# A sparse-attention decoder layer: when the cached rows for compression are gathered, and where two low parts of weights are made

## The chip, the cores and the metric

The kernel runs on one core of a Trainium2 chip. The metric is the device time of one execution in microseconds (us). The profile names the engines PE (TensorE, matmuls), PEld (its weight loads), DVE (VectorE), ACT (ScalarE), POOL (GpSimd) and SP (SyncE). SP and POOL issue all the transfers; these run on 16 DMA engines that both share.

## The reference, cut to what matters

One layer of a hybrid decoder: a projection of 1024 prompt tokens and 8 x 4 sample tokens, three attention branches (compressed blocks, selected blocks, window), a short convolution, and an output projection. The change touches the compression and the output projection:

```
def compress(kv, pe, w1, w2):                      # kv: (b, l, heads, 64), blocks of 64 rows
    blocks = kv.reshape(b, l // BLK, BLK, g, d) + pe[None, None, :, None, :]
    flat = blocks.transpose(0, 1, 3, 2, 4).reshape(b, l // BLK, g, BLK * d)
    return jax.nn.silu(flat @ w1) @ w2             # w1: (4096, 128), w2: (128, 64)
...
    k_cmp, v_cmp = compress(full(past_kc, kc), ...), compress(full(past_vc, vc), ...)
...
    o = jnp.concatenate([o_attn * silu(z_a), y_conv * silu(z_c)], axis=-1) @ w_out
    x = x + gate[:, None, :] * o
```

`past_kc` and `past_vc` are pages of two caches, picked by a page table: 8 sequences of 2048 rows of 128 numbers each.

## The kernel before, in words

Five engines run programs of their own, joined by semaphores. Each engine, and each engine's list of transfers, goes in the order in which the program is written; nothing is reordered.

**Stages.** Conditioning and key/value projection; the large input projection in 24 blocks `n` (a fast matrix product: seven products `i` = 0 to 6 a block in all but the first three); compression (`turn`, `pair`); prompt attention (units `u`); sample attention in four pairs of sequences `pq` = 0 to 3; the output projection of nine tiles `tt`.

**Compression.** `c` = 0 is the keys, `c` = 1 the values. For each, the cached rows come as four quarters `q` into the buffers `xq[0]` to `xq[3]`; a quarter is two indirect transfers (`T` = 0, 1) of 128 rows of 8 KB, 2.1 MB together. `xq[0]` lies in the tile `near`, so the profile gives it that name. All of these buffers lie where operands of the input projection were, and `gather_quarter(0, 0)` waits for a product of the last block. PE's `turn(c, t)`, `t` = 0 to 63, transposes 16 turns out of each quarter (lines 1311 and 1312; every eighth pair of turns begins with the prompt's rows, `xp4`, lines 1308 and 1310). DVE and ACT copy what was turned into `xt` (lines 2347 and 1872), and `pair(c, m)`, `m` = 0 to 31, multiplies it with the weights `w1` (line 1318). `turn(0, 0)` waits for quarter 0 and for all of `xp4[0]` (`xp_ld[0]` at 192); `turn(0, 16)`, `turn(0, 32)` and `turn(0, 48)` wait for quarters 1, 2 and 3; the step `m` = 8 waits for the last three quarters of `w1[0]` (`xp_ld[2]`). The buffer `xt1`, first written at `m` = 4, lies over `qp`, so DVE and ACT wait there for all stores of queries (`q_st`).

**What SP issues around it.** The first quarter of `w1[0]`, `load_rows(0, r)` for `r` = 0 to 3 (the prompt's rows and the position table into `xp4[0]`, lines 723 and 725), three more quarters of `w1[0]` (line 718); then, behind waits for the last product, for `ych_st` and for `q_st`, the same for `c` = 1.

**What POOL issues around it.** In the last block: `gather_quarter(0, 0)` at `i` = 2, `store_za(23, 1)` at `i` = 5 (line 984), `store_q(23, 0)` at `i` = 6 (line 992, four transfers). After the block: `store_za(23, 0)`, `store_q(23, 1)`, a wait for product 6, `gather_quarter(0, 1)`; then ten waits, among them those for all stores; two stores out of `tailr` (lines 1046 and 1047); and the other quarters.

**The end of the sample attention.** PE: `turn_rows(2)`, `pair_values(2)` (line 1589, ends with `o5_mm` = 3), `turn_rows(3, range(3))`, `turn_o(2)` (line 1595, waits for `o5_cp`), `turn_rows(3, range(3, 6))`, `pair_values(3)`, then the output projection (line 1632), whose step `k` of tile 0 waits for `m_lo`, `wo_hi` and `wo_lo`. DVE runs the list at lines 2571 to 2594: `wo_low(j)` (line 2473) makes the low part `wol[j]` of a block of output weights from what ACT made at line 1950, `combine(pq)` (lines 2528 to 2535) joins the branches and releases `turn_o`, `gate_rows` and `last_row_copies` (line 2563) follow PE, and `mix_low(0)` (line 2570) makes the low part of tile 0 from what ACT made at line 1989. `early(2)` is `range(3, 5)`, so two `wo_low`.

Of the kernel before, what the change touches and what calls it, by code (L numbers as in the profile page):

```python
# [52 lines left out]
NBLK, NPLAIN, NSLOT = 24, 3, 5  # L53
# [12 lines left out]
def build(nc: "bass.Bass", x_prompt, x_sample, cache_k_cmp, cache_v_cmp, cache_k_slc, cache_v_slc, cache_k_win,  # L66
# [24 lines left out]
    def f32(ap):  # L91
        return ap.bitcast(F32)

    with ctx:
# [282 lines left out]
        def early(pq):  # L377

            return (range(0), range(0, 3), range(3, 5), range(5, 16))[pq]
# [136 lines left out]
        def plain(n):  # L516
            return n < NPLAIN

        def products(n):
            return 8 if plain(n) else 7  # L520

        def product(n, i):

            return 8 * min(n, NPLAIN) + 7 * max(0, n - NPLAIN) + i
# [88 lines left out]
        def act_at(n, name):  # L613
            return p2_act, place(ACT_EV, n, name)
# [4 lines left out]
        def made(n, i):  # L619
            return p2_mm, product(n, i) + 1  # L620
# [47 lines left out]
        def rows_of(tt):  # L668
            return P if tt < NTT - 1 else SAMP
# [244 lines left out]
        def _(po):  # L914
# [20 lines left out]
            def store_bias(q):  # L935

                rv = rows
                po.dma_start(rowd[:, 16 * q:16 * q + 16, :], bass.AP(rv.tensor, rv.offset, [list(rv.ap[0]), [0, 16], [1, XW]])).then_inc(row_st, 16)

            po.wait_ge(kv_ev, 2 * NTT)  # L940
            def store_rows(which):

                dst, col, t0 = ((p_kc, C_KC, 0), (p_vc, C_VC, 0), (p_ks, C_KS, 0), (p_vs, C_VS, 0), (p_kw, C_KW, 4), (p_vw, C_VW, 4))[which]
                src = kvc[:, :, col:col + DKV] if which < 2 else kvt[:, t0:8, col - KOFF:col - KOFF + DKV]
                po.dma_start(dst.rearrange("l b (t p) g d -> p (l b t) (g d)", p=P), src).then_inc(kc_st if which < 2 else out_st, 16)
                nout[0] += 0 if which < 2 else 16
# [17 lines left out]
            def gather_quarter(c, q):  # L964
                if c == 0 and q == 0:
                    po.wait_ge(*made(NBLK - 1, 1))
                cache = (cache_k_cmp, cache_v_cmp)[c]
                src = cache.rearrange("l n (e t) g d -> (l n e) (t g d)", e=8)
                for T in range(2):
                    po.indirect_dma_start(xq[q][:, T, :], None, src, bass.IndirectOffsetOnAxis(idxq[:, T, q:q + 1], 0)).then_inc(xq_ld[q], 16)  # L970
# [6 lines left out]
            def store_conv(n, half):  # L977

                po.wait_ge(*dve_at(n, f"h{half}"))
                po.dma_start(mixd[8 + n // 3, :, half, :], yy[:, half, :]).then_inc(ych_st, 16)  # L980

            def store_za(n, half):
                po.wait_ge(*act_at(n, f"za{half}"))
                po.dma_start(zad[n // 3, :, half, :], (er if half == 0 and not plain(n) else ca[half])[:, :]).then_inc(zab_st[half], 16)

            def store_q(n, half):
                j = n // 3
                po.wait_ge(*dve_at(n, f"l{half}"))
                for g in range(2):
                    own, head, cols = slice(64 * g, 64 * g + 64), 4 * (j // 2) + 2 * g + j % 2, slice(HT * half, HT * half + HT)  # L990
                    for a in range(2):
                        po.dma_start(f32(qst[head, 64 * a:64 * a + 64, cols]), f32(qp[own, 2 * half + a, 0:HT])).then_inc(q_st, 16)

            for n in range(NBLK):
                for i in range(products(n)):
                    if plain(n):
                        if n == 0 and i == 1:
                            po.wait_ge(ada_ev, 8)
                            po.dma_start(gbd, gate[:, :]).then_inc(g_st, 16)
                        if n == 2:  # L1000
                            if i == 0:
                                store_conv(1, 1)
                            if i == 1:
                                store_conv(1, 0)
                            if i == 5:
                                store_za(n, 1)
                            if i == 6:
                                store_q(n, 1)
                            if i == 7:
                                store_za(n, 0)  # L1010
                    else:
                        if n % 3 == 0 and i == 0 and n > NPLAIN:
                            store_za(n - 1, 0)
                        if n % 3 == 0 and i == 2:
                            store_q(n - 1, 0 if n == NPLAIN else 1)
                        if n % 3 == 1 and i == 6:
                            store_conv(n, 0)
                        if n % 3 == 2:
                            if i == 1:
                                store_conv(n - 1, 1)  # L1020
                            if i == 5:
                                store_za(n, 1)
                            if i == 6:
                                store_q(n, 0)
                    if i == 2 and 2 <= n < 6:
                        store_rows(n)
                    if n < 2 and i % 2:
                        po.wait_ge(*made(n, i - 1))
                        store_bias(4 * n + i // 2)
                    if n == NBLK - 1 and i == 2:  # L1030
                        gather_quarter(0, 0)
            store_za(NBLK - 1, 0)
            store_q(NBLK - 1, 1)
            po.wait_ge(*made(NBLK - 1, 6))
            gather_quarter(0, 1)
            po.wait_ge(w_lo, N_OPERANDS)
            po.wait_ge(out_st, nout[0])
            po.wait_ge(ych_st, 32 * 8)
# [9 lines left out]
            for c in range(2):  # L1048
                for q in range(4):
                    if 4 * c + q >= 4:  # L1050
                        po.wait_ge(x3_t, 16 * (4 * c + q - 3))
                    if 4 * c + q >= 2:
                        gather_quarter(c, q)
            for q in range(4):
                po.wait_ge(xq_ld[q], 2 * 32)
# [976 lines left out]
        def _(dve):  # L2032
# [300 lines left out]
            for c in range(2):  # L2333
                for m in range(32):
                    n = 32 * c + m
# [135 lines left out]
            def wo_low(j):  # L2471
                dve.wait_ge(wo_hi, j + 1)
                dve.tensor_tensor(wol[j][:, :], wor[j][:, :], f32(woh[j][:, :]), ALU.subtract).then_inc(wo_lo, 1)
# [52 lines left out]
            def combine(pq):  # L2526
                dve.wait_ge(e5, pq + 1)
                link(dve.reciprocal(i5[:, :], r5[:, pq % 2, :]))
                link(dve.tensor_tensor(i5[:, :], i5[:, :], gr[:, pq, 1:3], ALU.mult))
                dve.wait_ge(o5_mm, pq + 1)  # L2530
                link(dve.tensor_scalar(o5[:, :], PS[:, 5, P:2 * P], i5[:, 0:1], None, ALU.mult))
                link(dve.scalar_tensor_tensor(o5[:, :], PS[:, 5, 2 * P:3 * P], i5[:, 1:2], o5[:, :], ALU.mult, ALU.add))
                dve.scalar_tensor_tensor(o5[:, :], PS[:, 5, 3 * P:4 * P], gr[:, pq, 0:1], o5[:, :], ALU.mult, ALU.add).then_inc(o5_cp, 1)
                dve.wait_ge(o5_cp, pq + 1)
                dve.sem_inc(b5_rd, 1)
# [22 lines left out]
            def last_row_copies():  # L2558
                dve.wait_ge(o5_mm, 3)
                for q in (1, 3, 5):  # L2560
                    n = 58 + q
                    dve.wait_ge(t5, n + 1)
                    dve.tensor_copy(pt5[:, 4 * q - 4:4 * q, :], PS[:, group_bank[n], :].rearrange("p (a c) -> p a c", a=4)).then_inc(ev5d, 1)

            def mix_low(tt, halves=(0, 1)):
                n = rows_of(tt)
                for a in halves:
                    dve.wait_ge(m_hi, 2 * tt + a + 1)
                    ks = slice(8 * a, 8 * a + 8)
                    dve.tensor_tensor(ml[:, ks, 0:n], mr[:, ks, 0:n], f32(mh[:, ks, 0:n]), ALU.subtract).then_inc(m_lo, 1)  # L2570
# [4 lines left out]
            for pq in range(2):  # L2575
# [4 lines left out]
                for j in early(pq):  # L2580
                    wo_low(j)
                pair_rows(pq + 2)
            for j in early(2):
                wo_low(j)
            combine(2)
            gate_rows(2)
            last_row_copies()
            mix_low(0)
            for j in early(3):
                if j == 10:  # L2590
# [106 lines left out]
```

## Time and profile before

| what | value |
|---|---|
| median of 3 runs | 1491.7 us (1487.86 to 1492.43) |
| the profiled execution | 1485.97 us |
| its span | 1484.2 us |
| PE busy | 1421.5 us, 96% of the span |
| DVE busy | 960.4 us, 65% |
| share of the 16 DMA engines' span | q1 23.1%, q0 15.1% |

The span is that of one profiled execution, from its first to its last record; its own device time is 1.8 us longer. q1 carries what SP issues, q0 what POOL issues. Shares of busy time are means over all stages; what a wait costs is read in its own stage.

### The profile page before, as it was taken

What the parts mean: (1) busy time and instruction counts of PE and PEld (TensorE: products, weight loads), DVE (VectorE), ACT (ScalarE), POOL (GpSimd) and SP (SyncE); (2) the same over time, 40 slices, a digit from 0 to 9 for tenths busy, and PEclk for the clock granted to TensorE, in tenths of its full rate; (3) what the DMA queues carried; (4) which work ended last, traced back from release to release, by engine and by line L of the source; (5) the groups of instructions that cost most, each with busy time, mean ns of one, the idle gap of its engine ahead of it and who ended that gap; (6) DMA issues with size and microseconds to landing.
All of it is one profiled execution on the core that took longest, in us unless ns stands there. A gap on an engine that the chain in (4) does not pass through costs nothing.

```text
span 1484.2 us, 27910 instructions
## 1 busy us (share of the span) xinstructions
PE 1421.5 (96%) x10526; PEld 1226.2 (83%) x10526; DVE 960.4 (65%) x2309; ACT 705.1 (48%) x1546; POOL 236.9 (16%) x447
## 2 busy tenths in 40 slices
PE   5999999999999999989989989989989999899998
PEld 1889999999999999977777777777777766688886
DVE  2646878878788787767676576576676563743226
ACT  2433233232322333266677777777777755621111
POOL 1101120110100101131021242232231141000000
PEclk9999999999999999999999999999999999999999
DMA  9335733332333423597221221221121049963321
GB/s 347 111 111 106 119 115 87 93 109 46 105 82 90 116 48 97 142 349 232 60 87 35 71 74 42 57 66 44 38 58 30 22 164 317 279 181 99 88 86 36
DMA packets 169862, 164.76 MB, mean 111 GB/s; under 512 B 53757, under 2 KB 150269, under 8 KB 164353
## 3 DMA queue, kind: packets, MB, share of 16 engines
q1 hardware_dynamic: 153904, 94.11, 23.1%
q0 software_dynamic: 15824, 68.87, 15.1%
q8 instruction: 84, 1.38, 0.4%
q14 instruction: 50, 0.40, 0.1%
HBM read 131.27 MB, written 35.83 MB: 113 GB/s over the span
## 4 chain that ended last, share of the span: by engine, by line
PE 88%; DVE 4%; DMA 3%; ACT 2%; issue 2%; SPq 1%; POOL 0%; DVEq 0%; ACTq 0%
PE PS L1266 33%; PE PS L1632 12%; PE PS L1438 8%; PE PS L1403 7%; PE PS L1382 5%; PE PS L1318 4%; PE PS L1383 4%; PE PS L1223 2%; PE PS L1224 2%; PE PS L1225 2%; DMA kwb<-in_cache_k_win 1%; DMA adaw<-in_ada_w 1%; PE PS L1485 1%; PE PS L1547 1%; PE PS L1414 1%
## 5 line engine op out<-in xcount | busy, mean ns | idle before, releaser
L1266 PEld LDWEIGHTS PS<-bo,wsl 128*128 128x128 f32 x4104 | 499.4, 188 | 0.4 <-issue 0.4
L1266 PE MATMUL PS<-bo,wsl 128*128 128x264 f32 x4104 | 499.6, 284 | 0.0
L1893 ACT ACTIVATE pr<-PS,nm 128x640 f32<-128x640 f32 (+7 forms) x256 | 181.3, 709 | 44.8 <-DVE nm L2395 42.2
L1728 ACT ACTIVATE wsl<-wsum 128x512 fp32r<-128x512 f32 x105 | 65.6, 631 | 237.8 <-DVE wsum L2118 237.8
L1916 ACT ACTIVATE ptt<-PS 128x512 f32<-128x512 f32 x264 | 149.8, 601 | 39.6 <-PE PS L1403 39.4
L1403 PE MATMUL PS<-ident,pr 128*128 128x128 f32 x1056 | 146.6, 273 | 0.3 <-ACT ptt L1916 0.3
L1438 PE MATMUL PS<-ptt,kvt 128*64 128x256 f32 x1056 | 136.2, 389 | 0.0
L1403 PEld LDWEIGHTS PS<-ident,pr 128*128 128x128 f32 x1056 | 122.1, 141 | 9.2 <-issue 0.6
L1438 PEld LDWEIGHTS PS<-ptt,kvt 128*64 128x64 f32 x1056 | 66.8, 136 | 41.1 <-issue 16.4
L2395 DVE CUSTOM_DVE_ANT_0 PS<-PS,near,nm 128x256 f32<-128x256 f32 x192 | 94.7, 493 | 6.8
L2394 DVE TENSOR_REDUCE nm<-PS 128x1 f32<-128x128 f32 (+5 forms) x128 | 70.5, 551 | 38.8 <-PE PS L1383 38.2
L2124 DVE TENSOR_TENSOR wsl<-wsum,wsl 128x512 fp32r<-128x512 f32 x105 | 70.9, 692 | 29.7 <-ACT wsl L1728 29.5
L1382 PE MATMUL PS<-ksh,qb 128*128 128x384 f32 (+3 forms) x192 | 75.9, 397 | 11.8 <-ACT pr L1893 10.5
L1632 PE MATMUL PS<-woh,mh 128*128 128x512 f32 x256 | 79.4, 391 | 0.0
L1632 PE MATMUL PS<-wol,mh 128*128 128x512 f32 x256 | 79.0, 390 | 0.0
L1632 PE MATMUL PS<-woh,ml 128*128 128x512 f32 x256 | 78.9, 389 | 0.0
L2570 DVE TENSOR_TENSOR ml<-mr,mh 128x1024 fp32r<-128x1024 f32 x16 | 19.6, 1226 | 90.7 <-ACT mh L1989 90.6
L1382 PE MATMUL PS<-kwh,qb 128*128 128x384 f32 (+3 forms) x192 | 70.8, 370 | 6.9 <-ACT pr L1893 6.9
L1318 PE MATMUL PS<-xt,w 128*128 128x273 f32 x256 | 72.1, 404 | 4.9 <-DVE xt L2347 2.6
L2118 DVE TENSOR_TENSOR wsum<-wr 128x512 f32<-128x512 f32 x105 | 68.5, 685 | 1.2 <-DMA wr<-in_w_in 1.2
L2347 DVE COPY xt<-PS 64x256 f32<-64x256 f32 x128 | 54.0, 422 | 23.3 <-PE PS L1312 19.5
L1989 ACT ACTIVATE mh<-mr 128x1024 fp32r<-128x1024 f32 x16 | 17.0, 1061 | 100.7 <-PE PS L1632 100.0
(358 smaller groups left out, 2422.0 us busy)
## 6 DMA issues: line engine op xcount, KB each, us to landing
wr<-in_w_in SPq DMA_DIRECT2D x32, 512.0 KB, 5.6
adaw<-in_ada_w SPq DMA_DIRECT2D x8, 1024.0 KB, 9.4
wr<-in_w_in SPq DMA_DIRECT2D x32, 256.0 KB, 4.5
q_stacked<-qp POOLq DMA_DIRECT2D x64, 128.0 KB
qb<-q_stacked SPq DMA_DIRECT2D x32, 256.0 KB, 3.0
mr<-mixed SPq DMA_DIRECT2D x16, 512.0 KB, 3.8
mixed<-yy POOLq DMA_DIRECT2D x16, 264.0 KB
xb<-in_x_prompt POOLq DMA_DIRECT2D x8, 512.0 KB, 4.5
```

The lines of the kernel that those rows point to most:

```text
L1266: ins = pe.matmul(PS[:, 2 * q + c, 0:H // 2], w[:, x, kk, :], b[:, y, kk, c * H // 2:(c + 1) * H // 2], start=(first and kk == 0 and x == ...
L1318: ins = pe.matmul(PS[:, 4 + g, 0:CB], w1[c][:, m, :], xt[m // 4 % 2][:, m % 4, g, :], start=(m == 0), stop=(m == 31))
L1382: pe.matmul(PS[:, b0 + c, x:x + m], q, kh[:, g, a:a + m], start=True, stop=False)
L1403: ins = pe.transpose(PS[:, turn_bank(c), h * P:(h + 1) * P], pr[w % 3][:, h, t * P:(t + 1) * P], ident[:, :])
L1438: ins = pe.matmul(PS[64 * g:64 * g + 64, 6, a:a + 2 * P], v, pt[tc % NPT5][:, 2 * g:2 * g + 2, :].rearrange("p j c -> p (j c)"), start=(t ...
L1632: ins = pe.matmul(PS[0:n, b0 + c, :], a[:, k, 0:n], b[k][:, 512 * c:512 * c + 512], start=(k == 0 and a is mh and b is woh), stop=(k == 15 ...
L1893: act.activation(pr[r][:, h, 0:k], score_cols(b0, w), ACT.Exp, scale=-1.0, bias=nm[:, r, h:h + 1], accum_out=rsum[:, r, h:h + 1]).then_inc ...
L1916: act.activation(pt[tc % NPT5][:, :, :], PS[:, turn_bank(c), :].rearrange("p (h c) -> p h c", h=4), ACT.Copy).then_inc(pt_act, 1)
L2118: dve.tensor_tensor(wsum[(sums_to(m) - 1) % 2][:, :, :], raw(*a), raw(*b), op).then_inc(w_sum, 1)
L2124: dve.tensor_tensor(wsl[m % NSLOT][:, 1, :, :], source(m), f32(wsl[m % NSLOT][:, 0, :, :]), ALU.subtract).then_inc(w_lo, 1)
L2394: link(dve.tensor_reduce(low, cols[:, 0:far], AX.X, ALU.min))
L2395: dve.tensor_tensor_reduce(cols[:, far:k], cols[:, far:k], near[:, head_of(u, h), 2 * P - (k - far):2 * P], 1.0, low if far else 3.0e38, A ...
```

## The change

Two things are moved; no work is added or left out.

- POOL: `gather_quarter(0, 1)` goes from behind the last product to the place `i` = 5 of the last block, behind a wait for product 4 alone; quarters 2 and 3 of the keys go from behind the stores' waits and the two `tailr` stores to the place where quarter 1 was. The values' quarters stay where they are.
- DVE: the two `wo_low` of `early(2)` go from in front of `combine(2)` to behind `last_row_copies()`, in front of `mix_low(0)`.

```
@@ -1029,10 +1029,14 @@
                     if n == NBLK - 1 and i == 2:
                         gather_quarter(0, 0)
+                    if n == NBLK - 1 and i == 5:
+                        po.wait_ge(*made(n, 4))
+                        gather_quarter(0, 1)
             store_za(NBLK - 1, 0)
             store_q(NBLK - 1, 1)
             po.wait_ge(*made(NBLK - 1, 6))
-            gather_quarter(0, 1)
+            gather_quarter(0, 2)
+            gather_quarter(0, 3)
             po.wait_ge(w_lo, N_OPERANDS)
             po.wait_ge(out_st, nout[0])
@@ -1049,7 +1053,7 @@
                 for q in range(4):
                     if 4 * c + q >= 4:
                         po.wait_ge(x3_t, 16 * (4 * c + q - 3))
-                    if 4 * c + q >= 2:
+                    if c:
                         gather_quarter(c, q)
@@ -2580,11 +2584,11 @@
                 pair_rows(pq + 2)
-            for j in early(2):
-                wo_low(j)
             combine(2)
             gate_rows(2)
             last_row_copies()
+            for j in early(2):
+                wo_low(j)
             mix_low(0)
```

## Rows read from the trace of the kernel before

**Rows 1.** The page: PE busy, and the chain by engine.

```profile
PE 1421.5 (96%) x10526; PEld 1226.2 (83%) x10526; DVE 960.4 (65%) x2309; ACT 705.1 (48%) x1546; POOL 236.9 (16%) x447
...
PE 88%; DVE 4%; DMA 3%; ACT 2%; issue 2%; SPq 1%; POOL 0%; DVEq 0%; ACTq 0%
```

**Rows 2.** Waits of PE, whole span: us in total, times, longest.

```profile
PE PS L1595 <- DVEq L2535: 2.0, 1, 2.0
...
PE PS L1308 <- DMA xp<-in_cmp_pe_k: 1.3, 1, 1.3
```

**Rows 3.** Timeline of POOL, 608 to 645: start, us, what, [idle before].

```profile
615.80 1.04 POOL L970 DMA_INDIRECT near<-in_cache_k_cmp,idxq  x1 [0.35 <-issue]
617.14 1.41 POOL L970 DMA_INDIRECT near<-in_cache_k_cmp,idxq  x1 [0.30 <-issue]
622.18 0.59 POOL L984 DMA_DIRECT2D z_attn_silu<-ca  x1 [3.63 <-ACT ca L1739]
625.84 2.14 POOL L992 DMA_DIRECT2D q_stacked<-qp  x4 [3.06 <-DVE qp L2196]
...
633.53 1.01 POOL L970 DMA_INDIRECT xq<-in_cache_k_cmp,idxq  x1 [0.30 <-issue]
...
639.24 0.57 POOL L1046 DMA_DIRECT2D out_p_cv<-tailr  x1 [3.41 <-DMA q_stacked<-qp]
```

**Rows 4.** DMA queues, 622 to 626: packets, MB, share of 16 engines.

```profile
q0 software_dynamic: 123, 1.00, 83.5%
q1 hardware_dynamic: 356, 0.23, 22.1%
```

**Rows 5.** DMA queues, 626 to 632.

```profile
q1 hardware_dynamic: 1504, 0.88, 82.5%
q0 software_dynamic: 153, 0.47, 29.6%
```

**Rows 6.** DMA queues, 638 to 642.

```profile
q0 software_dynamic: 216, 1.64, 99.2%
q1 hardware_dynamic: 117, 0.05, 4.8%
```

**Rows 7.** The chain, 600 to 765: start, us, what.

```profile
625.23 6.59 DMA xp<-in_cmp_pe_k
```

**Rows 8.** Timeline of PE, DVE and ACT, 624 to 650.

```profile
631.96 0.30 PE L1308 MATMUL PS<-ident,xp 128*128 128x128 f32 x1 [1.33 <-DMA xp<-in_cmp_pe_k]
...
634.23 2.16 PE L1318 MATMUL PS<-xt,w 128*128 128x273 f32 x4 [0.98 <-ACT xt L1872]
...
640.52 0.46 DVE L2345 COPY xt<-PS 64x68 f32<-64x68 f32 x2 [0.61 <-PE PS L1312]
...
645.03 1.09 PE L1318 MATMUL PS<-xt,w 128*128 128x273 f32 x4
...
646.69 0.86 DVE L2347 COPY xt<-PS 64x256 f32<-64x256 f32 x2 [2.18 <-PE PS L1312]
...
647.65 0.70 PE L1318 MATMUL PS<-xt,w 128*128 128x273 f32 x2 [0.83 <-DVE xt L2347]
```

**Rows 9.** Busy time by stretch: PE, PEld, DVE, ACT, POOL, PEclk, DMA share, GB/s.

```profile
634.00:638.00 4.00, 3.77 (x14) 3.18 (x15) 1.04 (x3) 0.94 (x4) 1.53 (x2) 0.57 1.10 370
...
1286.00:1290.00 4.00, 4.00 (x36) 3.34 (x36) 2.18 (x3) 2.67 (x4) 0.00 (x0) 0.57 1.13 348
```

**Rows 10.** Timeline of PE, 1262 to 1310.

```profile
1273.85 1.15 PE L1485 MATMUL PS<-ident,s 128*128 128x128 f32 x8 [0.19 <-ACT pt L1945]
...
1280.08 0.38 PE L1589 MATMUL PS<-vcs,pt 32*64 32x128 f32 x4
...
1283.82 0.30 PE L1595 MATMUL PS<-ident,o 128*128 128x128 f32 x1 [2.04 <-DVEq L2535]
...
1285.72 1.71 PE L1485 MATMUL PS<-ident,s 128*128 128x128 f32 x8 [1.16 <-DVE pt L2563]
...
1293.78 0.74 PE L1632 MATMUL PS<-woh,mh 128*128 128x512 f32 x2
```

**Rows 11.** Timeline of DVE, 1262 to 1310.

```profile
1279.82 2.36 DVE L2473 TENSOR_TENSOR wol<-wor,woh 128x1024 fp32r<-128x1024 f32 x2 [3.87 <-ACT woh L1950]
...
1282.49 0.35 DVE L2531 TENSOR_SCALAR o<-PS,i 128x128 f32<-128x128 f32 x1
...
1287.47 0.69 DVE L2563 COPY pt<-PS 128x512 f32<-128x512 f32 x1 [1.21 <-PE PS L1485]
1288.31 1.23 DVE L2570 TENSOR_TENSOR ml<-mr,mh 128x1024 fp32r<-128x1024 f32 x1
```

**Rows 12.** Timeline of ACT, 1262 to 1310.

```profile
1287.22 1.06 ACT L1989 ACTIVATE mh<-mr 128x1024 fp32r<-128x1024 f32 x1
```

**Rows 13.** Line 783 (last loads of window values, issued 1259.8 and 1260.1).

```profile
DMA to landing us min/median/max: 22.3/22.9/23.4
```

**Rows 14.** DMA queues, 632 to 638.

```profile
q1 hardware_dynamic: 2099, 1.06, 58.8%
q0 software_dynamic: 415, 1.20, 50.9%
```

More of the change, by code:

```diff
@@ L1031, in _ @@
                         gather_quarter(0, 0)
+                    if n == NBLK - 1 and i == 5:
+                        po.wait_ge(*made(n, 4))
+                        gather_quarter(0, 1)
             store_za(NBLK - 1, 0)
@@ L1034, in _ @@
             po.wait_ge(*made(NBLK - 1, 6))
-            gather_quarter(0, 1)
+            gather_quarter(0, 2)
+            gather_quarter(0, 3)
             po.wait_ge(w_lo, N_OPERANDS)
@@ L1051, in _ @@
                         po.wait_ge(x3_t, 16 * (4 * c + q - 3))
-                    if 4 * c + q >= 2:
+                    if c:
                         gather_quarter(c, q)
@@ L2582, in _ @@
                 pair_rows(pq + 2)
-            for j in early(2):
-                wo_low(j)
             combine(2)
@@ L2587, in _ @@
             last_row_copies()
+            for j in early(2):
+                wo_low(j)
             mix_low(0)
```

## The prediction

> **What bounds the kernel now.** The page comes first: PE is busy for 1421.5 of 1484.2 us and the chain lies on PE for 88% [rows 1]. PE's work isn't changed, so only its idle time and its clock can move: 62.7 us of idle time over the whole span, of which a change of order can reach a few. The waits of PE come second [rows 2]: they show which part of the change stands beside a wait. One wait, 2.0 us on DVE's line 2535, is the release of `turn_o(2)`, in front of which the two `wo_low` stand. No wait of PE names a quarter of the cached rows; the only wait on a transfer at the start of the compression is 1.3 us for `xp4`, which the diff doesn't touch. The third view, the timelines and the DMA queues around both places, gives the prices.
>
> **Part one, the quarters.** POOL's time first. Product 4 of the last block ends about when DVE starts on it, and POOL's `store_za(23, 1)` is issued until 622.77; then POOL is idle for 3.06 us until `store_q(23, 0)` [rows 3]. Two indirect transfers take 1.04 to 1.41 us each with 0.3 us ahead of them, so 2.7 to 3.4 us: quarter 1 fits in that hole, at a cost of 0 to 0.4 us to the stores behind it. Quarters 2 and 3 take four times 1.3 us from 633.5, until 638.8; POOL reached the first `tailr` store at 639.24, after waiting 3.41 us for the query stores [rows 3], so that issue is hidden too. What is now behind them in POOL's list, the `tailr` stores, is waited for by nothing until the end of the compression.
>
> What quarter 1 gains: `turn(0, 16)` follows `pair(0, 6)`. In the trace `pair(0, 7)` starts 2.62 us after it (645.03, 647.65), where 1.36 us is the pitch of the steps that wait for nothing (1.09 us of matmuls and two turns), and DVE stood idle for 2.18 us on PE's transposes [rows 8]. Something held PE for about 1.3 us where it comes to quarter 1, issued at 633.5 to 635.8 and so in flight for some ten us. I take it that this is the arrival of quarter 1, and that it goes: -1.3 us. The bound is 0, since the view names DVE and not the transfer. Quarters 2 and 3 gain nothing: PE shows no such hole at `turn(0, 32)` or `turn(0, 48)`.
>
> What quarter 1 costs. It puts 2.1 MB on q0 from 623 to 626, while the transfers of `xp4[0]`, with which PE starts, are on q1. The last of these is issued at 625.23 and takes 6.59 us [rows 7]; PE starts at 631.96 after its 1.33 us [rows 8], so any delay is PE's in full. The queues share the engines: while quarter 0 (8 KB rows) was on q0, q0 had 83.5% and q1 22.1%; once it was over, q1 had 82.5% [rows 4, 5]; and with quarter 1 alone q0 moved 1.64 MB in 4 us [rows 6]. So 2.1 MB take 5.1 us of all engines; while they run q1 keeps 22%, and the last of `xp4` comes 5.1 x 0.78 = 4.0 us later. Bounds: 0, if q1's packets hold their pace beside quarter 1, and 6.2 us, if q0 runs at the 1.00 MB in 4 us of [rows 4] (8.4 us for 2.1 MB, in which q1 does 1.9 of the 5.8 x 0.825 = 4.8 us of work that it has left at 626, and 3.6 us more for the rest, which makes 638.0). I take +4.0.
>
> The Trainium skill, "DMA: Bandwidth & Descriptors", section "Queues, rings and completion order", says that each DMA engine takes turns between the queues at packet granularity. By that rule, too, a queue of large rows holds up one of small rows, and it speaks against moving 2.1 MB in front of `xp4`; it gives no other sum.
>
> The clock: from 634 to 638 it stood at a mean of 0.57, 1.2 in place of 2.4 GHz for most of it, after the wait at line 1308 [rows 8, 9]; 4 us at 0.57 lose 1.7 us. If PE starts 4 us later, a stretch of the same length at the same place falls into waiting, and gives 1.7 us back; if it is longer or starts later, nothing. I take -0.8, with bounds of -1.7 and +1.7.
>
> Further waits that may come late. `q_st`: its stores are behind 2.1 MB more on q0; they were done before 639.24, DVE asks at 640.52, which moves to 644.5 [rows 3, 8]. So +0, up to +2 if they are later by over 5 us. `w1[0]`, q1: asked for at `m` = 8, near 649, without a wait. It now has quarter 1 in front of it and 4.2 MB of quarters 2 and 3 right behind the stores; beside such rows q1 had 4.8% [rows 6]. I take +0.5, bounds 0 and +3.
>
> Sum of part one: -1.3 + 4.0 - 0.8 + 0.5 = +2.4 us.
>
> **Part two, the low parts.** DVE was ready at 1275.95, waited 3.87 us for ACT's `woh`, and ran the two `wo_low` for 2.36 us; `combine(2)` read its first accumulator at 1282.49, and PE, idle for 2.04 us, went on at 1283.82 [rows 10, 11]. Without them `combine(2)` waits for `pair_values(2)` alone, which ends at 1280.46. From the first read to PE's start are 1.33 us, so PE starts at 1280.5 + 1.33 = 1281.85 and gains 1.95 us. The next wait, 1.16 us on the copies of `last_row_copies`, moves along as it is. Behind this, the clock: 0.57 from 1286 to 1290, after six us in which PE waited twice; eight transposes took 1.71 us where they took 1.15 before [rows 9, 10]. That cost 1.7 us. With one of the two waits gone I take it that it doesn't fall: -1.5 (bounds -1.7 and 0). The two `wo_low` now stand in front of `mix_low(0)`. DVE's last copy ended at 1288.16 and ends near 1285.6; two `wo_low` of 1.22 us end near 1288.1, and `mix_low(0)` can't start before ACT is done with `mh` at 1288.28, begun at 1287.22 [rows 11, 12]. So they are hidden, `m_lo` comes at 1289.6, and PE is there at 1293.78 - 3.45 = 1290.3. Without that cover they'd cost up to 2.4 us. `pair_values(3)` now starts near 1284.9, and the last values land at 1260.1 + 23.4 = 1283.5 [rows 13]: not late. Sum of part two: -3.4 us, between -1.9 and -3.7.
>
> **Sum.** +2.4 - 3.4 = -1.0 us on the profiled execution, 1485.97 to 1485.0 us. That execution is 5.7 us under the median of 1491.7 and 1.9 us under the lowest of the runs shown, so I take the difference over to the median: 1490.7 us.
>
> **The rivals.**
> - No measurable change (forecast): the parts cancel within 4.5 us. Within 0.3%, 4.5 us, is what a measurement of this kernel can't tell from none; the runs shown differ by that much.
> - Crowded out, slower: the place is `turn(0, 0)`. Quarter 1 holds `xp4` for the full 6.2 us, the same queue holds `w1[0]` for 3 us more at `m` = 8, the clock gives nothing, and part two gives 1.9: 6.2 + 3 - 1.3 - 1.9 = +6.0, 1497.7 us. For it: q1's 4.8% [rows 6]. Against: PE came to `m` = 8 without a wait. It decides once part one costs over 7.9 us, or over 6.4 with part two at its least.
> - Faster: `xp4` isn't held (cost 0), the hole at quarter 1 and both low stretches of the clock go: -1.3 - 1.7 - 3.5 = -6.5, 1485.2 us. For it: between 632 and 638, with stores and the first of quarter 1 on q0, both queues ran side by side at 58.8% and 50.9% [rows 14]. Against: [rows 4], where the large rows were alone on q0.
> - The change does nothing: both moves are hidden, since PE waits for no quarter by name and `combine(2)` waits for another thing. 1491.7 us, inside the forecast. Against: the 2.04 us [rows 2, 10].
>
> **How the numbers follow.** Forecast and the last rival together 0.62, crowded out 0.15, faster 0.23. The likeliest case's own range is 1487 to 1495. The range reaches to both outer cases: 1485.5 to 1497 leaves out the tails beyond them, and the scatter of the runs. Chances: faster by over 0.3% 0.22, within 0.63, slower 0.15.
>
> **What the profile would show.** `xq` for keys issued near 623, right behind line 984, and four more from 633.5; PE's wait at line 1308 grown from 1.3 to about 5 us, its first turn near 636; `pair(0, 7)` 1.4 us after `pair(0, 6)`; no wait of PE on line 2535, `turn_o(2)` right behind the transposes; no fall of the clock before the output projection, and DVE's `mix_low(0)` starting where it did relative to `mh`. Wrong it would be if line 1308 waits no longer than before (then faster), or if PE waits at `m` = 8 for `w1` or at line 1632 for `mix_low`.

## The result, and the profile after

The changed kernel takes 1493.44 us (median of 20 runs, 1489.7 to 1497.86) where the kernel before takes 1490.22 us (20 runs beside it, 1483.9 to 1493.15): ratio 1.003, 95% interval 1.002 to 1.0041, so 4.5 us slower (3.0 to 6.1). It stands at the edge of what was called no change, on the side that was given 0.15. The profiled execution took 1493.26 us, with a span of 1491.5 us. It is 7.3 us over the profiled execution of the kernel before, more than the 4.5 us of the runs, since that one was 4.3 us under its own median.

The waits of PE over the whole span of the changed kernel (us in total, times, longest), beside [rows 2]:

```profile
PE PS L1312 <- DMA xp<-in_cmp_pe_k: 7.1, 1, 7.1
...
PE PS L1489 <- DMA kb<-in_cache_k_slc,idxs: 2.1, 1, 2.1
...
PE PS L1315 <- DMA w<-in_cmp_w_k: 1.7, 1, 1.7
```

The wait on `combine(2)` is gone (the lines have moved by 4). The wait for `xp4` (line 1308 before, 1312 now) went from 1.3 to 7.1 us, and there is a new one for `w1` at `m` = 8.

The timeline of POOL, beside [rows 3]:

```profile
622.70 0.59 POOL L984 DMA_DIRECT2D z_attn_silu<-ca  x1 [3.66 <-ACT ca L1743]
623.59 0.97 POOL L970 DMA_INDIRECT xq<-in_cache_k_cmp,idxq  x1 [0.30 <-issue]
624.86 0.95 POOL L970 DMA_INDIRECT xq<-in_cache_k_cmp,idxq  x1 [0.30 <-issue]
626.36 2.19 POOL L992 DMA_DIRECT2D q_stacked<-qp  x4 [0.55 <-DVE qp L2200]
...
642.01 0.57 POOL L1050 DMA_DIRECT2D out_p_cv<-tailr  x1 [3.21 <-DMA q_stacked<-qp]
```

Quarter 1 is issued ten us earlier, and the stores behind it are issued on time: POOL still waits 0.55 us for DVE in front of them. Issuing costs nothing. The last store of queries was through at 642.0 in place of 639.2, and only POOL waited for it, no longer than before.

The timeline of PE, beside [rows 8] (the first turn, pairs 0, 3, 6 and 7, and the step `m` = 8):

```profile
638.21 0.45 PE L1312 MATMUL PS<-ident,xp 128*128 128x128 f32 x1 [7.07 <-DMA xp<-in_cmp_pe_k]
...
641.14 2.16 PE L1322 MATMUL PS<-xt,w 128*128 128x273 f32 x4 [0.56 <-ACT xt L1876]
...
648.34 1.09 PE L1322 MATMUL PS<-xt,w 128*128 128x273 f32 x4
...
652.72 1.09 PE L1322 MATMUL PS<-xt,w 128*128 128x273 f32 x4
...
654.30 1.09 PE L1322 MATMUL PS<-xt,w 128*128 128x273 f32 x4
657.04 0.33 PE L1315 MATMUL PS<-ident,xq 128*128 128x128 f32 x1 [1.65 <-DMA w<-in_cmp_w_k]
```

Busy time by stretch of the changed kernel (columns as in [rows 9]):

```profile
632.00:636.00 4.00, 0.00 (x0) 0.00 (x0) 0.47 (x1) 0.00 (x0) 3.39 (x6) 0.55 1.02 333
636.00:640.00 4.00, 1.79 (x9) 1.82 (x10) 0.85 (x3) 0.22 (x2) 2.20 (x3) 0.50 1.06 399
640.00:644.00 4.00, 3.44 (x12) 2.48 (x11) 1.29 (x4) 1.73 (x5) 1.12 (x2) 0.50 1.03 416
644.00:650.00 6.00, 5.95 (x32) 4.94 (x30) 3.30 (x9) 3.40 (x10) 0.00 (x0) 0.83 1.04 416
```

The clock fell while PE stood idle, as before, but it stayed at 1.2 GHz until about 646, eight us into the work. And the DMA queues (packets, MB, share of 16 engines), 628 to 636, while PE stands idle for `xp4`, then 632 to 638, 638 to 642 and 642 to 648:

```profile
q0 software_dynamic: 355, 2.35, 89.8%
q1 hardware_dynamic: 381, 0.24, 13.2%
...
q0 software_dynamic: 407, 1.91, 88.7%
q1 hardware_dynamic: 409, 0.22, 13.9%
...
q0 software_dynamic: 340, 1.47, 90.6%
q1 hardware_dynamic: 339, 0.17, 14.7%
...
q0 software_dynamic: 320, 2.33, 93.9%
q1 hardware_dynamic: 317, 0.16, 9.4%
```

The first column is what the prediction didn't look at: both queues have work, and each moves as many packets as the other, or nearly. q0's are mostly 8 KB rows (6.6 and 7.3 KB in the mean from 628 to 636 and from 642 to 648; 4.3 KB from 638 to 642, with stores among them), q1's 0.5 to 0.6 KB, so by bytes q0 gets about nine tenths.

The loss in this pair of traces can be laid out along PE's time. The tails come 0.51 us later in this trace (629.60 and 630.11), which is not the change's; against that offset:

| mark | later by, us | what was added |
|---|---|---|
| first turn | 5.74 | the wait for `xp4` |
| pair 3 | 7.19 | 1.45, the low clock |
| pair 7 | 6.14 | -1.05, the hole at quarter 1 closed |
| first pair behind the wait for `w1` | 7.49 | 1.35 |
| first scores of the prompt attention | 7.46 | 0 |
| output projection | 6.83 | -0.6, the low parts less other waits |

### The profile page after: what moved, and what is told of

Read it like the earlier page. It is cut to its first block, busy times and chain, and to the rows that moved or that the text cites. A ratio compares the mean times of both kernels' runs of the same rounds, so it can differ in the third digit from the quotient of the medians.

```text
span 1491.5 us, 27910 instructions
## 1 busy us (share of the span) xinstructions
PE 1423.5 (95%) x10526; PEld 1229.4 (82%) x10526; DVE 960.6 (64%) x2309; ACT 704.5 (47%) x1546; POOL 235.9 (16%) x447
## 4 chain that ended last, share of the span: by engine, by line
PE 86%; DMA 4%; DVE 4%; ACT 2%; issue 2%; SPq 1%; POOL 0%; DVEq 0%; ACTq 0%
PE PS L1270 33%; PE PS L1636 12%; PE PS L1442 8%; PE PS L1407 7%; PE PS L1386 5%; PE PS L1387 3%; PE PS L1322 3%; PE PS L1227 2%; PE PS L1228 2%; PE PS L1229 2%; DMA w<-in_cmp_w_k 2%; DMA kb<-in_cache_k_slc,idxs 1%; PE PS L1489 1%; DMA adaw<-in_ada_w 1%; PE PS L1593 1%
## 5 line engine op out<-in xcount | busy, mean ns | idle before, releaser
L1387 PE MATMUL PS<-ksl,qb 128*128 128x384 f32 (+3 forms) x192 | 64.1, 343 | 0.0
```

The costliest lines, as they stand in the source:

```text
L1387: ins = pe.matmul(PS[:, b0 + c, x:x + m], q, kl[:, g, a:a + m], start=False, stop=True)
```

## The experiments

Times are ratios to the kernel before, run beside on the same chip, with 95% intervals. 0.1% is 1.5 us.

**The quarters alone.** The changed kernel with the two `wo_low` back in front of `combine(2)`:

```
-            combine(2)
-            gate_rows(2)
-            last_row_copies()
             for j in early(2):
                 wo_low(j)
+            combine(2)
+            gate_rows(2)
+            last_row_copies()
```

> The quarters' part alone; the low parts stay in front of combine(2). Theory A (quarter 1 crowds out xp4): PE's first turn waits about 7 us for xp4, then about 1.7 us for w1 at m = 8, and half of the clock's low stretch falls on work: +7 to +8 us in the trace between the last product and the end of the compression, and +5 to +8 us in the time. Theory B (the loss seen came from elsewhere, such as the wait of 2.1 us for a key gather in the sample attention, and the quarters cost little): 0 to +3 us.

Measured: 1.0057 (1.0037 to 1.0078), so 8.5 us slower (5.5 to 11.6); waits of 6.5 us for `xp4` and 2.0 us for `w1`; the first scores 7.0 us later against the tails. Theory A, and B is out: this trace has no wait for a key gather in the sample attention at all.

**The low parts alone.** The kernel before with the second half of the diff:

> The low parts' part alone. Both theories: no wait of PE on combine(2) (2.0 us before) and PE at the output projection about 2 us earlier from turn_o(1) on; 3.4 us if the clock doesn't fall behind it. In the time -1.5 to -4 us. A rival, that the two wo_low now delay mix_low(0): 0 us, with a wait of PE at line 1632.

Measured: 0.9963 (0.9951 to 0.9976), so 5.5 us faster (3.6 to 7.3). PE's wait on `combine(2)` is gone; none on `mix_low` came. The gain is more than the 1.5 to 4 us expected. Within their intervals the two parts add up: +8.5 - 5.5 = +3.0, where both together gave +4.5 (3.0 to 6.1).

**Quarter 1 alone, and quarters 2 and 3 alone.** In the first, only this is added to the kernel before, with `gather_quarter(0, 1)` taken from its old place; in the second, quarter 1 stays and the other two follow it at once (and go from their old place):

```
# e3
+                    if n == NBLK - 1 and i == 5:
+                        po.wait_ge(*made(n, 4))
+                        gather_quarter(0, 1)
# e4
             po.wait_ge(*made(NBLK - 1, 6))
             gather_quarter(0, 1)
+            gather_quarter(0, 2)
+            gather_quarter(0, 3)
```

> Only quarter 1 is issued early; quarters 2 and 3 stay behind the waits for the stores. Theory A: the whole wait at line 1308 is here (6.5 to 7.5 us), the wait for w1 at m = 8 may be gone; +5 to +7 us in the time. Theory C (it is all 6.3 MB together that hold up q1): the wait at line 1308 is under 4 us and the time +1 to +3 us.

> Quarter 1 stays behind the last product, quarters 2 and 3 are issued right behind it, in front of the waits for the stores. Theory A: the wait at line 1308 is 1.3 us as before, since nothing is added to q0 before 633; w1 comes later and PE may wait for it at m = 8, 0 to 3 us: 0 to +3 us in the time. Theory C: +3 to +6 us.

Measured: quarter 1 alone 1.0029 (1.0016 to 1.0042), so 4.3 us slower (2.4 to 6.3), somewhat less than was expected, with 6.1 us of wait for `xp4` and none for `w1`; quarters 2 and 3 alone 1.0005 (0.9988 to 1.0022), 0.7 us of wait for `xp4`. The wait for `xp4` is quarter 1's. The two don't add up to the quarters' 8.5 us; but the intervals are wide enough to hold the 3.4 us left over. Part of it is the wait for `w1` of 1.7 to 2.0 us, which is in both traces with all three quarters moved and in neither of these. The second trace names a wait at quarter 1, which the trace of the kernel before did not (waits of PE, 610 to 760):

```profile
PE PS L1310 <- DMA xq<-in_cache_k_cmp,idxq: 1.2, 1, 1.2
PE PS L1310 <- DMA xp<-in_cmp_pe_k: 0.7, 1, 0.7
```

**Half of quarter 1.** Only the first of its two transfers is early, the second at the old place:

```
-            def gather_quarter(c, q):
+            def gather_quarter(c, q, halves=(0, 1)):
...
+                        gather_quarter(0, 1, (0,))
...
             po.wait_ge(*made(NBLK - 1, 6))
-            gather_quarter(0, 1)
+            gather_quarter(0, 1, (1,))
```

> The dose: only the first of quarter 1's two transfers (1.05 MB) is early, the second stands where quarter 1 was, and quarters 2 and 3 as before. Theory A by bytes: PE's wait at line 1308 lies half way between 1.3 and 6.3 us, 3 to 5 us. A theory in which any large row on q0 starves q1 until the stores are through gives 6 us as with the whole quarter; one of a threshold gives 1.3.

Measured, one run of 1493.28 us: a wait of 4.1 us. With 1.3 us for nothing early, 4.1 for 1.05 MB and 6.1 for 2.1 MB, the wait grows with the bytes in front.

**The rows first.** In the changed kernel, and in the kernel with the low parts alone, the rows of `xp4` go in front of the first quarter of `w1[0]`:

```
-            load_w1(0, 0, wr_ld)
             sp.wait_ge(kc_st, 32)
             for r in range(4):
                 load_rows(0, r)
+            load_w1(0, 0, wr_ld)
```

> The changed kernel, with load_rows(0, r) issued in front of the first quarter of w1[0]. Theory A (quarter 1's 2.1 MB hold up whatever of q1 is still due): the wait only moves, from xp4 (7.1 us) to w1 at the first pair; pair 0 starts 0 to 2 us earlier than in the changed kernel and the time is 0 to -2 us against it, so +2 to +5 us against before. Theory D (xp4 is slow for its own small rows and its order behind w1): xp4's wait falls under 3 us, nothing takes its place, and the time is no more than +1 us against before.

> The low parts' part with the quarters as before, and load_rows(0, r) in front of the first quarter of w1[0]. Nothing of quarter 1 is on q0 here before 633. Theory D: the 1.3 us of wait at line 1308 go, so -1 to -1.5 us against e2_lowparts. Theory A: w1's first quarter becomes the one that comes last, 0 to +1 us against e2_lowparts. Either way between -4 and -7 us against before.

Measured in the changed kernel: 1.0085 (1.0057 to 1.0113), worse than either theory had it. Waits of PE, 610 to 765:

```profile
PE PS L1315 <- DMA w<-in_cmp_w_k: 11.5, 1, 11.5
PE PS L1312 <- DMA xp<-in_cmp_pe_k: 3.6, 1, 3.6
```

`xp4` came earlier by 3.5 us. But `w1`'s first 512 KB, which were in before PE asked for them in the changed kernel, were now in only at 648.7, and pair 0 began at 649.59. What of q1 is left when quarter 1 begins goes one packet for each of q0's, until q0 runs out of 8 KB rows; there are 1024 packets of 512 bytes in a quarter of `w1` and 256 rows in a quarter of the cache. With the low parts alone the same order of loads did nothing: 0.9969 (0.9948 to 0.999), pair 0 at 632.85, no wait for `xp4` or `w1`, and a wait of 2.0 us for quarter 1 in their place.

**PE kept busy.** To take the clock away from the wait:

```
             tails()
+            for k in range(56):
+                pe.transpose(PS[:, 5, 0:P], ident[:, :], ident[:, :])
             turn(0, 0)
```

> The changed kernel with 56 transposes of the identity (about 6 us of PE) between tails and turn(0, 0), into a bank that pair 0 overwrites: it separates the wait from the clock. The transfers are the same, so the first turn starts within 0.5 us of where it does in the changed kernel. If the clock is a price of its own, the first four steps run at the full clock, pair 7 comes 3 to 4 us earlier, and the time is -2 to -4 us against the changed kernel unless w1 at m = 8 then takes it back as a longer wait (1.7 us now, 4 to 5 us then), in which case the time is the same.

Measured: 1.0049 (1.0026 to 1.0073), so nothing won. The clock held at 1.00 until pair 6, which came at 647.79 in place of 652.72. But (timelines of POOL and PE):

```profile
648.61 1.00 POOL L970 DMA_INDIRECT near<-in_cache_v_cmp,idxq  x1 [6.45 <-PE PS L1316]
...
663.98 0.48 PE L1315 MATMUL PS<-ident,xq 128*128 128x128 f32 x1 [13.52 <-DMA w<-in_cmp_w_k]
```

PE was through quarter 0 earlier, POOL gathered the values' first quarter at 648.61 in place of 653.53, and this closed the gap in q0 in which `w1` had landed. In the wait of 13.5 us the clock fell after all, from 654 to 667, the last 3.5 us of it on work. So this run doesn't take the clock's price out of the time; it moves it to the next wait. **The same with that gather held back:**

```
+                    if 4 * c + q == 4:
+                        po.wait_ge(xp_ld[2], 48)
                     if c:
                         gather_quarter(c, q)
```

> The kernel of e7 (changed kernel, PE kept busy), with the values' quarter 0 issued only once w1[0] has landed whole. Theory E (while 8 KB rows are on q0 the engines take one packet of each queue in turn, so 512-byte packets of w1 get through only one for each 8 KB row; in e7 the values' quarter, issued at 648.6, closes the hole in q0 in which w1 would have landed): PE's wait at m = 8 falls from 13.5 us to 5 to 8 us, w1 lands near 657, and the time is 5 to 7 us under e7. Theory F (w1 is late for its own sake, by the rate of 512-byte packets): the wait stays over 11 us.

Measured: 1.0022 (1.0000 to 1.0043), and a wait of 7.4 us in place of 13.5, as theory E has it; theory F is out. The time is 4.0 us under that with PE kept busy alone, where 5 to 7 were expected, and the two intervals overlap, so the times by themselves don't show the gain. The queues from 648 to 654 in this kernel:

```profile
q1 hardware_dynamic: 2132, 1.11, 76.6%
q0 software_dynamic: 155, 0.68, 28.0%
```

With few rows on q0, q1 moves 2132 packets in six us, where it moved 310 from 642 to 648.

**The opposite of the change.** With the low parts, quarter 1 held until `w1[0]` is in:

```
             po.wait_ge(*made(NBLK - 1, 6))
+            po.wait_ge(xp_ld[2], 48)
             gather_quarter(0, 1)
```

> The low parts' part, and the opposite of the change to the quarters: quarter 1 is issued only once w1[0] has landed whole. Theory E: without 8 KB rows on q0, w1 is through near 638 to 640 in place of 646 to 647; quarter 1 takes 5 to 6 us and lands near 645 to 646, where PE asks for it, so the hole of 1.3 us there is gone or is now a wait of 0 to 2 us for quarter 1; quarters 2 and 3 are still in time. 0 to -2 us against the low parts alone. Theory F: w1 is as late as before, quarter 1 comes after 651 and PE waits for it over 4 us: +4 us or more.

Measured: 1.0000 (0.9985 to 1.0015), a miss: 3.3 to 5.5 us above the two measurements of the low parts alone. `w1` was in at 640.2, but that was hardly a gain: in the kernel before, q1 moved only 16 packets from 640 to 642 beside 116 of q0, so it had little left by then, and the expectation's 646 to 647 was wrong. And PE then waited:

```profile
PE PS L1309 <- DMA xq<-in_cache_k_cmp,idxq: 6.4, 1, 6.4
```

Quarter 1, issued from 640.23, took eleven us to land and not five to six. The `tailr` stores and the other quarters were issued right behind it; that they are the reason was not tested. Both ends are bad; the place where the kernel before has this gather lies between them.

**PE kept busy for 1.3 us, and the low parts again.** The same loop with 12 in place of 56 on the kernel with the low parts, and that kernel once more:

> The low parts' part with 12 transposes of the identity (1.3 us) in the wait at line 1308. If the clock's fall at the start of the compression is a price of its own: it comes later or not at all, and 1 to 3 us against the low parts alone. Theory E's objection: PE then comes sooner to m = 8 and waits for w1, so nothing is gained (0 to +1 us).

> The kernel of e2 again, to set e10 and e11 beside it on the same chip: 0.9963 of before again within 0.0015, PE's wait on combine(2) absent.

Measured: 0.9965 (0.9947 to 0.9982) and 0.9978 (0.9952 to 1.0003): no difference. With the short loop PE waited 2.9 us for quarter 1. The low parts alone remain the best version, at 0.9963 and 0.9978, though the second interval just reaches the kernel before. Their second trace is the one in which nothing else happened near the end of the sample attention, so the prediction's second part can be read from it (timeline of PE):

```profile
1281.16 0.30 PE L1595 MATMUL PS<-ident,o 128*128 128x128 f32 x1
...
1289.55 0.73 PE L1632 MATMUL PS<-woh,mh 128*128 128x512 f32 x2
```

## Why the prediction was wrong, step by step

**POOL's issue, right.** Quarter 1 fitted in the hole, quarters 2 and 3 too; `q_st` wasn't waited for late.

**The hole at quarter 1, right in size, not in what it was due to.** Taken at -1.3 us, measured -1.05. Waits of 1.2 to 2.9 us for `xq` in four experiments with quarter 1 at its old place show that PE can come there too early. But in the first trace of the low parts, with quarter 1 at its old place too, PE came to pair 6 at 646.28 in place of 645.03, and pair 7 followed 1.58 us later, without a hole and as in the changed kernel (timeline of PE, pairs 6 and 7):

```profile
646.28 1.09 PE L1318 MATMUL PS<-xt,w 128*128 128x273 f32 x4
...
647.86 1.09 PE L1318 MATMUL PS<-xt,w 128*128 128x273 f32 x4
```

A PE that comes a little over one us later has no hole, moved or not. The prediction itself made PE 4 us late at `xp4`, and that alone would have closed the hole: the -1.3 belongs in the sum, but as part of the delay and not as a gain of the early issue. That the hole in the trace of the kernel before was quarter 1's arrival is likely, not shown.

**The wait for `xp4`, mis-sized: the first of the two terms that failed.** Taken at +4.0 with bounds of 0 and 6.2, measured at +5.7. The step was "2.1 MB take 5.1 us of all engines; while they run q1 keeps 22%". Both halves were too kind. q0 moved 2.35 MB in the eight us from 628 to 636, nearer the rate of [rows 4] than that of [rows 6], and q1 had 13.2% of the engines meanwhile. The 22% was read in [rows 4], where q0 moved 123 packets and q1 356: by these counts it was no stretch of two full queues. In one, q1 has as many packets as q0, and 9 to 15% in the stretches shown above. The kernel before shows this too: in the second half of [rows 4] itself, 624 to 626, and later, from 654 to 660 and from 660 to 666.

```profile
q0 software_dynamic: 70, 0.57, 88.5%
q1 hardware_dynamic: 82, 0.06, 11.4%
...
q0 software_dynamic: 251, 1.82, 92.6%
q1 hardware_dynamic: 251, 0.13, 9.8%
...
q0 software_dynamic: 324, 2.37, 96.7%
q1 hardware_dynamic: 324, 0.07, 5.9%
```

**The clock, wrong in sign: the second, and by size the larger miss.** Taken at -0.8, measured +1.45, so 2.25 us off where `xp4` was 1.7. The step was "a stretch of the same length at the same place falls into waiting". A longer wait didn't swallow the low stretch, it made it longer: 634 to 638 before, 632 to 646 now. The experiments agree: the stretch at 1.2 GHz behind the wait for `xp4` was absent after waits of 0.7 and 0.9 us, nought to 7 us long after 1.3 to 1.5, 7 us after 4.1 and 10 to 14 us after 6.1 to 7.1; with PE kept busy in place of the wait it was absent there. What its removal would be worth in the time was not measured, as the run with PE kept busy only came sooner to `w1` and lost the clock there.

**`w1` at `m` = 8, too small.** Taken at +0.5, measured +1.35, within its bounds. All of part one is then +7.5 in place of +2.4. That is the rival "crowded out", by its own mechanism, with less of a wait for `w1` than it had and a price of the clock that it left out; it had 0.15 and 1497.7 us. I gave each term its middle, although the clock hangs on the wait for `xp4`, and that wait and the one for `w1` on the same shares of the same queues, so that they move together.

**The low parts, right.** Taken at -3.4. From `turn_o(1)` to the output projection PE gained 3.54 us in the trace of the low parts' second run (-0.69 to -4.23 against before), of it 1.97 at `combine(2)`, and the clock didn't fall; the times gave -5.5 and -3.3 us. From `turn_o(2)` to the output projection PE took 8.4 us in all nine traces with the part, at the full clock, and 9.9 to 11.5 in the five without it, where the clock fell behind the wait. `mix_low` hid the two `wo_low`. In the changed kernel's own trace the gain from `turn_o(1)` on was 1.69 us: a wait of 2.1 us for a key gather stood in front, with a low stretch of the clock behind. Such a wait, 0.7 to 3.4 us, is in eight of the fourteen traces and absent from the others, with and without either part; what decides it was not found.

**The sum.** -1.0 us was forecast and +4.5 measured; the traces give +7.5 for the quarters and -1.7 to -3.5 for the low parts. 1493.44 us lies in the range, but only because that was wide: part two came as forecast, part one cost three times its forecast.

## What to carry to other kernels

A transfer issued earlier is not free because its buffer is free and its engine idle: here it took its share from what was due next, and with its larger pieces nearly all. Before such a move, list what is still due on the other queue, count it in packets, and look whether a wait stands on it. Read the queues' shares in a stretch where the counts show that both were full, and a gain at a wait only against the time at which the engine will come there after the change. Terms that hang on one resource fail together, so their sum has a wide tail on one side, and it belongs in the chances.

## What the runs showed of the hardware

With work on both queues, the engines moved about one packet of the one for each packet of the other: 340 to 339, 320 to 317, 324 to 324, 309 to 310, with mean sizes from 4.3 to 7.3 KB on q0 and 0.2 to 0.5 KB on q1. That left 6 to 15% of the engines' time for the small ones, and their rate fell from some 350 packets a us (2132 in six us) to 50 (310 in six us). The Trainium skill, "DMA: Bandwidth & Descriptors", section "Queues, rings and completion order", has the engines take turns by packets of several descriptors; the packets that this profile counts took turns one by one. Whether they are the page's packets or its descriptors, no run here shows.
